# The seam between two transformer blocks, worked in two halves of the tokens

## The chip, the cores and the metric

The kernel runs on one core of a Trainium2 chip. The metric is the device time of one execution in microseconds (us), as the median of several runs. Five engines work side by side, each through its own instructions in a fixed order, and they wait for each other by semaphores: TensorE (PE: matmuls, and its weight loads, PEld), VectorE (DVE), ScalarE (ACT), GpSimd (POOL) and SyncE (SP, which here only starts transfers).

## The reference

Two blocks stand one behind the other, on 512 tokens of width 1024. Cut to what surrounds the seam:

```python
# end of the first block
x = x + 0.5 * swiglu(rmsnorm(x, ffn2_norm), ffn2_w_gate, ffn2_w_up, ffn2_w_down)
x = rmsnorm(x, final_norm)
# start of the second block
h = rms_norm(x, mix_pre_g) * (1.0 + sc_m) + sh_m
p = h @ w_in                     # 1024 -> 2848 columns
p_conv, p_rw = p[..., :2 * CONV_WIDTH], p[..., 2 * CONV_WIDTH:]
# ... shift by one token, and the low-rank products of tanh(wd), ad, sigmoid(gd)
```

`swiglu` ends in the "second down projection", 2816 -> 1024. `sc_m` and `sh_m` come from a modulation that is computed earlier.

## The kernel before

**Layout.** Activations lie transposed: features on the 128 partitions, the 512 tokens along the free axis, so `xT` is eight tiles of 128x512 (`KD = 8` row blocks). All products are made in three passes of split numbers (`passes`, lines 606 to 608: weight high by activation high, weight high by activation low, weight low by activation high), so each 128-deep step k of a row block costs three matmuls, each with a weight load of 128x128.

**Weights.** They come as slabs of 128x1024 through a ring of four (`RING`). SyncE starts the transfer of slab n when `slab_done` says that slab n-4 is used up. GpSimd splits each slab into `w_hi` (line 540) and `w_lo` (line 542) and signals `w_split`. A row block of the down projection takes three slabs (steps 0-7, 8-15, 16-21), a row block of the next projection ("in2", 23 row blocks) takes one.

**The seam.** `down("down2", ...)` (line 759) makes eight row blocks into banks 0 to 3 of PSUM in turn. VectorE adds each to `xT` (line 1829, `x_new`), ScalarE squares it (line 1329, and once more scaled by the final gain, line 1333), VectorE sums the squares (lines 1709 and 1714). The sums over features are taken by TensorE (`stat`, line 685). The two norms are folded: three sums per token give the factor of both norms together (`both_rs`) and that of the first alone (`n_rs`). Behind the last row block the chain is:

- TensorE `last_sums` with the squares of the last block; ScalarE two roots (lines 1373, 1374); VectorE two reciprocals (1720, 1722); TensorE `spread` (line 696), four transposes that lay `both_rs` over all partitions in bank 6;
- for each j of 8: VectorE scales `xT` (line 1754), ScalarE adds the shift and rounds to `h_hi` (line 1392), VectorE makes `h_lo` (line 1744), in a ping-pong over two tiles;
- TensorE `first(2, ...)` (lines 636, 637, 642) takes each j as it comes, for the first two slabs of in2, interleaved by k. Then it spreads `n_rs` into bank 5, and goes on with `project(2)`, `project(3)`, ...

```python
            first(2, at, "mixpre", lambda n: pe.wait_ge(S("x_new"), 21 + n))
            for m in range(2, 23):
                project(m)
                if 3 <= m <= 8:
                    lora_products(2 * (m - 3), 2 * (m - 3) + 2)
```

**Behind the seam.** The spread of `n_rs` lets VectorE finish the first norm in place (`final_norm`, line 2221, eight operations, `x_final`). Only then VectorE's fixed order comes to four memsets (2227) and the token shift of the first three row blocks (`shifted`, line 2014); ScalarE then applies tanh and two sigmoids (1627 to 1629, `lora_act`). The first low-rank product (line 1052), which stands in TensorE's order right behind `project(3)`, waits for both:

```python
                    if n == 0:
                        pe.wait_ge(S("lora_in"), 48)
                        pe.wait_ge(S("lora_act"), 3)
                        pe.wait_ge(S("masks_made"), 12)
                    ...
                    if n == 0:
                        pe.wait_ge(S("x_final"), 8)
```

The order of the work is written out by hand on every engine; nothing is planned at build time.

## Time and profile before

| | us |
|---|---|
| median of 3 runs (1737.14 to 1739.49) | 1737.27 |
| the profiled execution's own time | 1742.76 |
| its span | 1740.7 |
| PE busy | 1684.3 (97%) |
| POOL busy | 1017.7 (58%) |
| DVE busy | 976.7 (56%) |
| ACT busy | 428.6 (25%) |

The page's busy shares are means over a program of many stages. Of the slices (section 2 of the page), TensorE's granted clock stands at nine tenths or more nearly throughout, with three slices at eight tenths, none of them here. For this change one stretch of some 50 us matters, from the last row block of the down projection (its first matmul starts at 980.20) to the first low-rank product (1027.98). Times of the trace are counted from the start of the span.

### The profile page before, as it was taken

The numbers are of one execution on the slowest core, as the hardware profiler recorded it, in microseconds if no ns is written. First come the engines' busy times: TensorE is split into PE (matmuls) and PEld (weight loads), VectorE is DVE, ScalarE is ACT, GpSimd is POOL, SyncE is SP. The second block draws the span as 40 slices with busy tenths as digits, with TensorE's granted clock in tenths as the row PEclk, the third lists the DMA queues.
The fourth block names the chain that finished last, engine by engine and source line by source line (L and its number), as shares of the span: only waits on it lengthen the run. The fifth ranks groups of instructions, "written<-read, shape, count | busy, mean of one in ns | idle before, by whom it ended". The sixth has DMA issues, their size and how long they took to land.

```text
span 1740.7 us, 26685 instructions
## 1 busy us (share of the span) xinstructions
PE 1684.3 (97%) x10126; PEld 1363.6 (78%) x10126; DVE 976.7 (56%) x1413; ACT 428.6 (25%) x708; POOL 1017.7 (58%) x607
## 2 busy tenths in 40 slices
PE   8999999999989999999999999989999899999998
PEld 6888888887755678888888777878878788888886
DVE  6666661237566346566662269987746676556102
ACT  4000000017845321111100131323433333333001
POOL 3666667766576567666677644630005476666775
PEclk9999999999999999999999999999989899999998
DMA  6444443332220134444443322210002133323333
GB/s 214 156 145 144 145 145 109 99 125 91 79 68 2 37 104 145 145 145 145 145 157 99 107 84 73 94 40 3 3 2 85 61 97 96 96 96 96 105 101 109
DMA packets 49518, 173.76 MB, mean 100 GB/s; under 512 B 5632, under 2 KB 6016, under 8 KB 49312
## 3 DMA queue, kind: packets, MB, share of 16 engines
q1 hardware_dynamic: 40464, 143.00, 25.1%
q10 hardware_dynamic: 8976, 29.63, 5.3%
q8 instruction: 60, 0.98, 0.2%
q14 instruction: 18, 0.15, 0.0%
HBM read 170.51 MB, written 2.10 MB: 99 GB/s over the span
## 4 chain that ended last, share of the span: by engine, by line
PE 88%; DVE 5%; ACT 2%; POOL 2%; issue 1%; DMA 1%; SPq 0%; ACTq 0%; DVEq 0%; POOLq 0%
PE banks L606 24%; PE banks L608 24%; PE banks L607 24%; PE banks L1017 4%; PE banks L685 1%; POOL prob L549 1%; PE banks L917 1%; PE banks L636 1%; PE banks L903 1%; PE banks L642 1%; PE banks L637 1%; DMA w_raw<-in_slabs 1%; PE banks L992 1%; DVE tmp_r L1893 1%; PE banks L677 0%
## 5 line engine op out<-in xcount | busy, mean ns | idle before, releaser
L540 POOL TENSOR_SCALAR w_hi<-w_raw 128x1024 fp32r<-128x1024 f32 x260 | 294.2, 1131 | 645.6 <-DMA w_raw<-in_slabs 644.6
L542 POOL TENSOR_TENSOR w_lo<-w_raw,w_hi 128x1024 fp32r<-128x1024 f32 x260 | 643.0, 2473 | 21.7
L606 PE MATMUL banks<-h_hi,w_hi 128*128 128x512 f32 x1376 | 540.1, 392 | 2.3 <-POOL w_lo L542 2.3
L608 PE MATMUL banks<-h_hi,w_lo 128*128 128x512 f32 x1376 | 535.5, 389 | 0.0
L607 PE MATMUL banks<-h_lo,w_hi 128*128 128x512 f32 x1376 | 535.4, 389 | 0.0
L606 PEld LDWEIGHTS banks<-h_hi,w_hi 128*128 128x128 f32 x1376 | 258.3, 188 | 61.8 <-issue 5.8
L607 PEld LDWEIGHTS banks<-h_lo,w_hi 128*128 128x128 f32 x1376 | 258.3, 188 | 54.3 <-issue 1.7
L608 PEld LDWEIGHTS banks<-h_hi,w_lo 128*128 128x128 f32 x1376 | 258.3, 188 | 54.4
L606 PE MATMUL banks<-act_hi,w_hi 128*128 128x512 f32 x528 | 205.6, 389 | 0.0
L608 PE MATMUL banks<-act_hi,w_lo 128*128 128x512 f32 x528 | 205.4, 389 | 0.0
L607 PE MATMUL banks<-act_lo,w_hi 128*128 128x512 f32 x528 | 205.4, 389 | 0.0
L1781 DVE TENSOR_TENSOR act_lo<-tmp,act_hi 128x512 f32 x66 | 111.3, 1687 | 8.1
L608 PEld LDWEIGHTS banks<-act_hi,w_lo 128*128 128x128 f32 x528 | 99.1, 188 | 20.7
L607 PEld LDWEIGHTS banks<-act_lo,w_hi 128*128 128x128 f32 x528 | 99.1, 188 | 20.7
L606 PEld LDWEIGHTS banks<-act_hi,w_hi 128*128 128x128 f32 x528 | 99.1, 188 | 20.2
L1789 DVE TENSOR_TENSOR tmp<-banks,tmp 128x512 f32<-128x512 f32 x44 | 30.4, 692 | 149.5 <-PE banks L608 145.7
L1398 ACT ACTIVATE tmp<-tmp 128x512 f32<-128x512 f32 x44 | 27.9, 634 | 331.8 <-DVE tmp L1789 331.7
L1829 DVE SCALAR_TENSOR_TENSOR xT<-banks,xT 128x512 f32<-128x512 f32 x24 | 16.5, 690 | 164.2 <-PE banks L608 164.2
L549 POOL TENSOR_SCALAR prob<-prob,small 128x128 f32<-128x128 f32 (+3 forms) x64 | 69.4, 1100 | 27.0 <-DVE small L1967 26.8
L1803 DVE CUSTOM_DVE_ANT_0 adaw<-adaw,silc 128x1024 f32<-128x1024 f32 x48 | 78.2, 1629 | 5.6 <-DMA adaw<-in_ada 5.3
L2338 DVE SCALAR_TENSOR_TENSOR tmp<-banks,vec,tmp 128x511 f32<-128x511 f32 x44 | 32.8, 746 | 64.1 <-ACT tmp L1681 63.8
L1794 DVE TENSOR_TENSOR tmp<-tmp 128x512 f32<-128x512 f32 x44 | 62.1, 1410 | 8.5 <-ACT tmp L1398 8.5
(363 smaller groups left out, 1914.2 us busy)
## 6 DMA issues: line engine op xcount, KB each, us to landing
w_raw<-in_slabs SPq DMA_DIRECT2D x262, 512.0 KB, 3.5
adaw<-in_ada ACTq DMA_DIRECT2D x48, 512.0 KB, 3.7
relb<-in_relb ACTq DMA_DIRECT2D x8, 256.0 KB, 2.9
out_y<-xT SPq DMA_DIRECT2D x8, 256.0 KB, 2.1
w_raw<-in_slabs SPq DMA_DIRECT2D x4, 256.0 KB, 5.0
xT<-in_x SPq DMA_DIRECT2D x1, 1024.0 KB, 8.2
block<-in_block ACTq DMA_DIRECT2D x1, 704.0 KB, 6.2
xT<-in_x SPq DMA_DIRECT2D x2, 256.0 KB, 3.7
```

The lines of the kernel that those rows point to most:

```text
L540: nc.gpsimd.tensor_scalar(w_hi[:, r, :], w_raw[:, r, :], 1.0, 1.0, ALU.mult, ALU.mult).then_inc(S("w_hi"), 1)
L542: nc.gpsimd.tensor_tensor(w_lo[:, r, :], w_raw[:, r, :], w_hi[:, r, :], ALU.subtract).then_inc(S("w_split"), 1)
L549: nc.gpsimd.tensor_scalar(p, p, of_step(row_sum, t)[:, e:e + 1], None, ALU.mult).then_inc(S("probs_normed"), 1)
L606: mm(out, hi, rhs_hi, start=start, stop=False, skip_group_check=True)
L607: mm(out, hi, rhs_lo, start=False, stop=False, skip_group_check=True)
L608: return mm(out, lo, rhs_hi, start=False, stop=stop, skip_group_check=True)
L1017: last = mm(out, block_of(lhs, operands, e, g, c), r, start=opens and i == 0, stop=i == len(pairs) - 1, skip_group_check=True)
L1781: v.tensor_tensor(actl_t[:, bass.ds(at * T, T)], t, hi, ALU.subtract).then_inc(S("act_lo"), 1)
L1789: v.tensor_tensor(tmp[:, 2 + u, :], bank[2 * u], tmp[:, 0, :], ALU.mult).then_inc(S("gate_scaled"), 1)
L1794: v.tensor_tensor(tmp[:, 4 + u, :], tmp[:, 2 + u, :], tmp[:, 4 + u, :], ALU.mult)\
L1803: v.tensor_tensor_reduce(out=adaw[:, u, :], in0=adaw[:, u, :], in1=silc, scale=1.0, scalar=0.0, op0=ALU.mult, op1=ALU.add, accum_out=mod_s ...
L2338: v.scalar_tensor_tensor(out=tmp[:, n, 1:T], in0=bank[n][:, 0:T - 1], scalar=w[1], in1=tmp[:, n, 1:T], op0=ALU.mult, op1=ALU.add).then_inc ...
```

## The change

The last row block of the down projection, the norm chain and the first three slabs of in2 are worked for tokens 0-255 first and for tokens 256-511 after them.

- TensorE: `last_row_of_down2` makes the row block as two halves (bank 3 and bank 2), each with all 22 steps, with the statistics and the spread of half 0 put between the steps of half 1. `first_of_in2` makes slabs 0, 1, 2 for half 0, slab behind slab, with the statistics and the spread of half 1 in slab 0, and then slabs 0, 1, 2 for half 1. The ring's `slab_done` comes only in the second half of each. The spread of `n_rs` stands behind all six. `project` begins with m = 3.
- VectorE: `pre_halves` runs scale and `h_lo` by halves (16 pairs for 8), with the sum (`pre_sum`) and the root (`pre_root`) of half 1 between those of half 0.
- ScalarE: squares, roots and `h_hi` by halves; the start of two small transfers stands between `h_hi` of half 0 and of half 1.
- Semaphore counts behind it are shifted by one (`root_of`, `squares_before`, ...); no other work moves.

The core of the diff:

```diff
@@ TensorE @@
+            def last_tile_sums(half):
+
+                pe.wait_ge(S("norm_square"), squares_before("mixpre") + 8 + half)
+                for t in (2 * half, 2 * half + 1):
+                    last = mm(bank[7][:, 3 * t:3 * t + 3], tmp[:, 1, P * t:P * t + P], of_last, start=False, stop=True,
+                              skip_group_check=True)
+                last.then_inc(S("norm_stat"), 1)
+
+            def both_spread(half):
+
+                pe.wait_ge(S("both_rs"), half + 1)
+                for t in (2 * half, 2 * half + 1):
+                    last = nc.tensor.transpose(bank[6][:, P * t:P * t + P], both_rs[:, t:t + 1].to_broadcast([P, P]), ident)
+                last.then_inc(S("second_mm"), 1)
+
+            def last_row_of_down2():
+
+                def part(half, s, k0, k1):
+                    n = SLAB_AT["down2"] + 3 * (KD - 1) + s
+                    return product(bank[3 - half][:, tokens_of(half)], n, n % RING, act_hi, act_lo, ks=range(k0, k1), start=k0 == 0,
+                                   stop=k1 == KF, at_slab=k0 - DOWN_CUT[s][0], tokens=tokens_of(half))
+
+                pe.wait_ge(S("x_new"), 16 + KD - 4)
+                part(0, 0, 0, 8)
+                part(0, 1, 8, 16)
+                part(0, 2, 16, KF - 1)
+                sums_of_most("mixpre")
+                part(0, 2, KF - 1, KF).then_inc(S("half_mm"), 1)
+                pe.wait_ge(S("x_new"), 16 + KD - 1)
+                part(1, 0, 0, 4)
+                last_tile_sums(0)
+                part(1, 0, 4, 6)
+                both_spread(0)
+                part(1, 0, 6, 8).then_inc(S("slab_done"), 1)
+                part(1, 1, 8, 16).then_inc(S("slab_done"), 1)
+                part(1, 2, 16, KF).then_inc(S("slab_done"), 1)
+
+            def first_of_in2(at):
+
+                def part(half, n, k0, k1):
+                    for k in range(k0, k1):
+                        if k == 0:
+                            if half == 0:
+                                pe.wait_ge(S("x_new"), 25 if n == 2 else 21 + n)
+                            pe.wait_ge(S("w_split"), at + n + 1)
+                        done = 8 * (HI_AT["mixpre"] + half) + k + 1
+                        w, r, out = slice(P * k, P * k + P), (at + n) % RING, bank[n][:, tokens_of(half)]
+                        pe.wait_ge(S("norm_hi"), done)
+                        mm(out, w_hi[:, r, w], h_hi[:, k, tokens_of(half)], start=k == 0, stop=False, skip_group_check=True)
+                        mm(out, w_lo[:, r, w], h_hi[:, k, tokens_of(half)], start=False, stop=False, skip_group_check=True)
+                        pe.wait_ge(S("norm_lo"), done)
+                        last = mm(out, w_hi[:, r, w], h_lo[:, k, tokens_of(half)], start=False, stop=k == KD - 1, skip_group_check=True)
+                    return last
+
+                part(0, 0, 0, 3)
+                last_tile_sums(1)
+                part(0, 0, 3, 6)
+                both_spread(1)
+                part(0, 0, 6, 8)
+                part(0, 1, 0, 8)
+                part(0, 2, 0, 8)
+                for n in range(3):
+                    part(1, n, 0, 8).then_inc(S("slab_done"), 1)
+                pe.wait_ge(S("norm_rs"), root_of("mixpre") + 1)
+                spread(bank[5], n_rs, 1).then_inc(S("norm_spread"), 1)
...
-            first(2, at, "mixpre", lambda n: pe.wait_ge(S("x_new"), 21 + n))
-            for m in range(2, 23):
+            first_of_in2(at)
+            for m in range(3, 23):
                 project(m)
@@ ScalarE @@
+            pre_square(0)
+            pre_std(0)
+            pre_hi(0, range(6))
+            pre_square(1)
+            pre_hi(0, (6,))
+            pre_std(1)
+            pre_hi(0, (7,))
             for i in range(2):
                 act.dma_start(lora[:, i, :], lora_in[:, i, :]).then_inc(S("lora_in"), 16)
-            norm_hi("mixpre")
+            pre_hi(1, range(KD))
@@ VectorE @@
+            def pre_halves():
+
+                sum_squares("mixpre", 6)
+                pre_sum(0)
+                pre_root(0)
+                for half in range(2):
+                    pre_scaled(half, 0)
+                    pre_scaled(half, 1)
+                    for j in range(KD):
+                        pre_lo(half, j)
+                        if j + 2 < KD:
+                            pre_scaled(half, j + 2)
+                        if half == 0 and j == 3:
+                            pre_sum(1)
+                        if half == 0 and j == 5:
+                            pre_root(1)
+                dve.wait_ge(S("norm_std"), root_of("mixpre") + 1)
+                v.reciprocal(n_rs, n_std).then_inc(S("norm_rs"), 2)
...
-            norm_split("mixpre", gs["mixpre"])
+            pre_halves()
```

How the instructions move. First place, TensorE, the start of in2. The names are PSUM banks, the split activations (`h_hi`, `h_lo`) and the split slab (`w_hi`, `w_lo`). Before:

```order
L696 MATMUL banks<-both,small 128x128 [waits both_rs]
L696 MATMUL banks<-both,small 128x128 x3
L636 MATMUL banks<-h_hi,w_hi 128x512 [waits norm_hi,w_split,x_new]
L637 MATMUL banks<-h_hi,w_lo 128x512
L636 MATMUL banks<-h_hi,w_hi 128x512 [waits w_split,x_new]
L637 MATMUL banks<-h_hi,w_lo 128x512
L642 MATMUL banks<-h_lo,w_hi 128x512 [waits norm_lo]
L642 MATMUL banks<-h_lo,w_hi 128x512
```

Now, from step k = 2 of slab 0, half 0:

```order
L786 MATMUL banks<-h_hi,w_hi 128x256 [waits norm_hi]
L787 MATMUL banks<-h_hi,w_lo 128x256
L789 MATMUL banks<-h_lo,w_hi 128x256 [waits norm_lo]
L742 MATMUL banks<-small,tmp 128x3 [waits norm_square]
L742 MATMUL banks<-small,tmp 128x3
L786 MATMUL banks<-h_hi,w_hi 128x256 [waits norm_hi]
L787 MATMUL banks<-h_hi,w_lo 128x256
L789 MATMUL banks<-h_lo,w_hi 128x256 [waits norm_lo]
```

Before, each step served two slabs with six matmuls of 512 columns behind one pair of waits; now a step serves one slab with three matmuls of 256 columns, and the statistics of half 1 stand among them.

Second place, TensorE, around the spread of `n_rs` (line 696 before, 706 now). Before:

```order
L642 MATMUL banks<-h_lo,w_hi 128x512
L696 MATMUL banks<-both,small 128x128 [waits norm_rs]
L696 MATMUL banks<-both,small 128x128 x3
L606 MATMUL banks<-h_hi,w_hi 128x512 [waits w_split]
L607 MATMUL banks<-h_lo,w_hi 128x512
L608 MATMUL banks<-h_hi,w_lo 128x512
```

Now:

```order
L789 MATMUL banks<-h_lo,w_hi 128x256 [waits norm_lo]
L706 MATMUL banks<-both,small 128x128 [waits norm_rs]
L706 MATMUL banks<-both,small 128x128 x3
L618 MATMUL banks<-h_hi,w_hi 128x512 [waits w_split]
L619 MATMUL banks<-h_lo,w_hi 128x512
L620 MATMUL banks<-h_hi,w_lo 128x512
```

Before, 48 matmuls (slabs 2 and 3) stood between the spread and the first low-rank product; now 24 do (slab 3), since slab 2 stands ahead of the spread.

Third place, VectorE, the middle of half 0 (scale at line 1867, `h_lo` at 1874, the sum of half 1 at 1850). Now:

```order
L1874 SCALAR_TENSOR_TENSOR h_lo<-tmp,mod,h_hi 128x256 [waits norm_hi]
L1867 SCALAR_TENSOR_TENSOR tmp<-xT,mod,banks 128x256 [waits norm_lo]
L1850 SCALAR_TENSOR_TENSOR xT<-banks,xT 128x256 [waits slab_done]
L1874 SCALAR_TENSOR_TENSOR h_lo<-tmp,mod,h_hi 128x256 [waits norm_hi]
L1867 SCALAR_TENSOR_TENSOR tmp<-xT,mod,banks 128x256 [waits norm_lo]
```

The sum of half 1 waits for the end of the down projection, and four `h_lo` of half 0 (with two scalings between them) are still behind it in VectorE's order, the first of them j = 4. Before, no such wait stood inside the sequence.

## Rows read from the trace of the kernel before

**Rows 1.** the page: busy time by engine, and the chain that ended last.
```profile
PE 1684.3 (97%) x10126; PEld 1363.6 (78%) x10126; DVE 976.7 (56%) x1413; ACT 428.6 (25%) x708; POOL 1017.7 (58%) x607
...
PE 88%; DVE 5%; ACT 2%; POOL 2%; issue 1%; DMA 1%; SPq 0%; ACTq 0%; DVEq 0%; POOLq 0%
```

**Rows 2.** stretches: us, busy of PE, PEld, DVE, ACT, POOL, then PEclk, DMA.
```profile
980.20:1016.07 35.87, 32.19 (x143) 25.80 (x142) 17.36 (x26) 7.93 (x14) 17.09 (x10) 0.90 0.24 74
1000.40:1007.20 6.80, 5.11 (x14) 3.35 (x13) 5.82 (x7) 2.22 (x4) 3.42 (x2) 0.50 0.23 77
1050.90:1100.00 49.10, 49.10 (x203) 37.97 (x203) 47.99 (x74) 5.66 (x9) 25.93 (x16) 1.00 0.23 76
```

**Rows 3.** TensorE in time: start us, us, engine, line, tiles, shape, count [idle].
```profile
994.02 0.39 PE L607 MATMUL banks<-act_lo,w_hi 128*128 128x512 f32 x1
994.25 0.39 PE L608 MATMUL banks<-act_hi,w_lo 128*128 128x512 f32 x1
994.48 1.84 PE L685 MATMUL banks<-small,tmp 128*128 128x2 f32 x16
996.18 0.49 PE L606 MATMUL banks<-act_hi,w_hi 128*128 128x512 f32 x1
...
998.58 1.05 PE L685 MATMUL banks<-small,tmp 128*128 128x3 f32 x8 [1.44 <-ACT tmp L1329]
...
1002.83 0.77 PE L636 MATMUL banks<-h_hi,w_hi 128*128 128x512 f32 x1 [1.69 <-ACT h_hi L1392]
...
1016.07 0.60 PE L696 MATMUL banks<-both,small 128*128 128x128 f32 x4
...
1021.98 0.39 PE L606 MATMUL banks<-h_hi,w_hi 128*128 128x512 f32 x1
...
1027.98 0.70 PE L1052 MATMUL banks<-in_arena 64*128 64x512 f32 x2 [0.40 <-issue]
```

**Rows 4.** TensorE in time, attention stage: two and three transposes.
```profile
505.02 0.44 PE L903 MATMUL banks<-both,prob 128*128 128x128 f32 x2
...
559.75 0.55 PE L903 MATMUL banks<-both,prob 128*128 128x128 f32 x3
```

**Rows 5.** VectorE in time order, around the seam.
```profile
1002.72 2.10 DVE L1744 SCALAR_TENSOR_TENSOR h_lo<-tmp,mod,h_hi 128x512 fp32r<-128x512 f32 x1
...
1005.52 0.75 DVE L1744 SCALAR_TENSOR_TENSOR h_lo<-tmp,mod,h_hi 128x512 fp32r<-128x512 f32 x1
...
1006.97 0.75 DVE L1744 SCALAR_TENSOR_TENSOR h_lo<-tmp,mod,h_hi 128x512 fp32r<-128x512 f32 x1
...
1016.77 5.36 DVE L2221 SCALAR_TENSOR_TENSOR xT<-xT,vec,banks 128x512 f32<-128x512 f32 x8 [1.97 <-PE banks L696]
1022.09 0.56 DVE L2227 MEMSET in_arena<- 128x32 f32 x4
1022.68 1.41 DVE L2014 SCALAR_TENSOR_TENSOR in_arena<-banks,vec,in_arena 128x511 f32<-128x511 f32 x2
1024.01 0.74 DVE L2014 SCALAR_TENSOR_TENSOR tmp<-banks,vec,tmp 128x511 f32<-128x511 f32 x1
```

**Rows 6.** GpSimd in time order: the two halves of one slab split.
```profile
1000.77 1.04 POOL L540 TENSOR_SCALAR w_hi<-w_raw 128x1024 fp32r<-128x1024 f32 x1 [2.28 <-DMA w_raw<-in_slabs]
1001.90 2.37 POOL L542 TENSOR_TENSOR w_lo<-w_raw,w_hi 128x1024 fp32r<-128x1024 f32 x1
```

**Rows 7.** groups by shape: busy us, mean ns, idle; one operation, two widths.
```profile
L1958 DVE CUSTOM_DVE_ANT_0 prob<-banks,relb 128x512 f32<-128x512 f32 x8 | 5.2, 688 | 2.6 <-PE banks L883 2.6
...
L1958 DVE CUSTOM_DVE_ANT_0 prob<-banks,relb 128x256 f32<-128x256 f32 x8 | 3.1, 422 | 0.1
```

**Rows 8.** ScalarE in time order, before the first low-rank product.
```profile
1024.78 0.64 ACT L1627 ACTIVATE in_arena<-in_arena 64x512 f32<-64x512 f32 x1 [0.61 <-DVE tmp L2014]
...
1027.27 0.61 ACT L1629 ACTIVATE tmp<-tmp 128x512 f32<-128x512 f32 x1
```

**Rows 9.** the page: slab transfers, count, size, median us to landing.
```profile
w_raw<-in_slabs SPq DMA_DIRECT2D x262, 512.0 KB, 3.5
```

More of the change, by code:

```diff
@@ L344, in build @@
         mod_sum = small_t[:, 236:237]
-        pre_ms, pre_std, pre_rs = (small_t[:, 24 + 4 * i:28 + 4 * i] for i in range(3))
+        pre_ms, pre_std_at, pre_rs = (small_t[:, 24 + 4 * i:28 + 4 * i] for i in range(3))
         gain_q = small_t[:, 200:203]
@@ L608, in passes, with product @@
                 return mm(out, lo, rhs_hi, start=False, stop=stop, skip_group_check=True)
-            def product(out, n, r, act_h, act_l, ks=range(KD), first=0, start=True, stop=True, wait_k=None, at_slab=0):
+            def product(out, n, r, act_h, act_l, ks=range(KD), first=0, start=True, stop=True, wait_k=None, at_slab=0,
+                        tokens=slice(None)):
                 pe.wait_ge(S("w_split"), n + 1)
@@ L619, in product @@
                     a, b = start and i == 0, stop and i == len(ks) - 1
-                    last = passes(out, hi, lo, act_h[:, first + k, :], act_l[:, first + k, :], a, b)
+                    last = passes(out, hi, lo, act_h[:, first + k, tokens], act_l[:, first + k, tokens], a, b)
                 return last
@@ L648, in first @@
                     norm_stats(late)
-                elif norm == "mixpre":
-                    pe.wait_ge(S("norm_rs"), NORMS.index(norm) + 1)
-                    spread(bank[5], n_rs, 1).then_inc(S("norm_spread"), 1)
             def first_loaded(wait_bank):
@@ L727, in norm_spread @@
             def norm_spread(name):
-                q = NORMS.index(name)
+                q = root_of(name) - 1
                 pe.wait_ge(S("norm_rs"), q + 1)
@@ L761, in down @@
                 at = SLAB_AT[name]
-                for m in range(KD):
+                for m in range(KD - 1 if norm == "mixpre" else KD):
                     if m >= 4:
@@ L772, in down @@
                         wait_k = (lambda k: pe.wait_ge(S("act_lo"), o + 3 + k)) if m == 0 else None
-                        early = norm in ("mixpre", "ffnpost") and m == KD - 1 and s == 2
+                        early = norm == "ffnpost" and m == KD - 1 and s == 2
                         if early:
@@ L782, in down @@
                     return
+                if norm == "mixpre":
+                    last_row_of_down2()
+                    return
                 last_sums(norm)
-                if norm == "mixpre":
-                    pe.wait_ge(S("both_rs"), 1)
-                    spread(bank[6], both_rs, 1).then_inc(S("second_mm"), 1)
-                else:
-                    norm_spread(norm)
+                norm_spread(norm)
             gate_up("gu1", 0, "ffn1")
@@ L1329, in square @@
                     f(tmp[:, j % 2 if j else 4, :], at, ACT.Square).then_inc(S("norm_square"), 1)
-                    if name == "mixpre" and j < KD - 1:
+                    if name == "mixpre":
                         if j >= 3:
@@ L1357, in norm_squares @@
                 else:
-                    for j in range(KD):
+                    for j in range(KD - 1 if name == "mixpre" else KD):
                         if name == "ffn2" and j == KD - 1:
@@ new lines, in pre_root, with pre_scaled @@
+            def pre_root(half):
+                cols = slice(2 * half, 2 * half + 2)
+                dve.wait_ge(S("second_std"), half + 1)
+                v.reciprocal(both_rs[:, cols], both_std[:, cols]).then_inc(S("both_rs"), 1)
+            def pre_scaled(half, j):
+                h, n = slice(HALF * half, HALF * half + HALF), 8 * (HI_AT["mixpre"] + half)
+                if j == 0:
+                    dve.wait_ge(S("second_mm"), half + 1)
+                    dve.wait_ge(S("x_new"), 16 + KD + half)
+                if j >= 2:
+                    dve.wait_ge(S("norm_lo"), n + j - 1)
+                v.scalar_tensor_tensor(out=tmp[:, 4 + j % 2, h], in0=xT[:, j, h], scalar=gs["mixpre"][:, j:j + 1], in1=bank[6][:, h],
+                                       op0=ALU.mult, op1=ALU.mult).then_inc(S("norm_t"), 1)
@@ new lines, in pre_lo @@
+            def pre_lo(half, j):
+                h = slice(HALF * half, HALF * half + HALF)
+                dve.wait_ge(S("norm_hi"), 8 * (HI_AT["mixpre"] + half) + j + 1)
+                v.scalar_tensor_tensor(out=h_lo[:, j, h], in0=tmp[:, 4 + j % 2, h], scalar=shf["mixpre"][:, j:j + 1],
+                                       in1=h_hi[:, j, h], op0=ALU.add, op1=ALU.subtract).then_inc(S("norm_lo"), 1)
+            def pre_halves():
[15 more added lines that the diff above has]
+                v.reciprocal(n_rs, n_std).then_inc(S("norm_rs"), 2)
+                dve.wait_ge(S("norm_rs"), root_of("mixpre") + 1)
@@ L1824, in add_half @@
             def add_half(o, at, n_slabs, scale, norm):
-                for m in range(KD):
+                for m in range(KD - 1 if norm == "mixpre" else KD):
                     sum_squares(norm, m - 1)
@@ L2315, in _ @@
             post_scaled(0)
-            dve.wait_ge(S("norm_std"), NORMS.index("ffnpre") + 1)
-            v.reciprocal(pre_rs, pre_std).then_inc(S("norm_rs"), 1)
+            dve.wait_ge(S("norm_std"), root_of("ffnpre"))
+            v.reciprocal(pre_rs, pre_std_at).then_inc(S("norm_rs"), 1)
             post_added(0)
```

90 lines of the change are left out of this document (49 added, 41 removed).

## The prediction

> **What bounds the kernel now.** The page first: TensorE is busy for 97% of the span and carries 88% of the chain that ended last [rows 1]. So a change pays only where TensorE waits, runs at the lower clock, or does less; it does not do less here. The views of stretches and of time around the seam show what there is to win. From 980.20 (last row block of the down projection) to the spread at 1016.07 TensorE is busy 32.2 of 35.9 us, and from 1000.40 to 1007.20 its granted clock is 0.50, that is 1.2 instead of 2.4 GHz, behind a gap in which it had only the short statistics and four transposes to do [rows 2, 3]. Between the row block's end (three matmuls from 996.18) and the first matmul of in2 (1002.83) lie about 5.9 us; the matmuls from 1002.83 to 1007.20 ran at the lower clock, which cost half of 4.4, so 2.2. About 7 us is the most that halves can win.
>
> Next the reader is to look behind the seam. The first low-rank product starts at 1027.98 with 0.40 idle ahead of it [rows 3]. It waits for VectorE: spread at 1016.07, final norm 1016.77 to 1022.09, four memsets, three shifts to 1024.75 [rows 5], then tanh from 1024.78 and two sigmoids, of which the last ends at 1027.88 [rows 8]. That chain is 11.91 us long from the spread on, and TensorE has just enough to do meanwhile: four transposes and two slabs. It has no slack.
>
> **The change, part by part.**
>
> *Matmul count and pitch.* 66 (22 steps) and 72 (three slabs of 8) matmuls of 512 columns become 276 of 256 columns, with as many weight loads. At 512 columns one starts every 0.227: two starts are 0.23 apart, and 24 x 0.227 + 4 x 0.11 = 5.89 of the 5.91 us between 1016.07 and 1021.98 [rows 3]. No row has 256 columns with a full weight load. From below: half of it is 0.113, and a weight load with next to nothing behind it already takes 0.106 (16 in 996.18 - 994.48 = 1.70) [rows 3], with a transpose 0.11 (0.55 for three less 0.44 for two) [rows 4]. From above: 512 columns at 2.4 GHz are 0.213; if the surplus of 0.013 comes with each matmul, 256 columns take 0.107 + 0.013 = 0.120. I take the middle, 0.117: 276 x 0.117 = 32.3 for 138 x 0.227 = 31.3, so +1.0 (0 to +1.8).
>
> A rule speaks against that. The rows show a weight load hidden under the matmul before it: load alone 0.106, matmul alone 0.213, together 0.227 [rows 3]. The Trainium skill, "TensorE: Matmul & The Clock Gate", section "What overlaps and what doesn't", says that a weight load overlaps matmuls in flight only where the row groups differ; here they are the same, so the trace disagrees at 512 columns, and what is left of it is the rival below. The same page's section "Back-to-back issue gap" gives N/2.4 + 2.5 ns: by it 256 columns take an estimated 0.109, and the sum would be 276 x 0.109 = 30.1, 2.2 less than mine; at 512 columns it gives 0.216, and the rows have 0.227.
>
> *Statistics and spreads.* 16 + 4 + 4 weight-load pairs x 0.111 = 2.7 and 4 transposes x 0.11 = 0.4: the same number as before, at other places.
>
> *The spread of n_rs with no wait at all.* 980.20 + 32.3 + 2.7 + 0.4 = 1015.6. It must stand behind all three slabs now; before, it stood behind two, at 1016.07. So even a perfect overlap moves it by only -0.5 (-1.5 to +0.3 with the pitch).
>
> *Waits in slab 0.* Half 0 of the row block ends at 980.2 + 7.7 + 1.8 + 0.3 = 989.9 or so; sum, square, statistics, root and spread at half width put the first h_lo at about 994. Before, one h_lo followed another by 1.45 (1005.52 to 1006.97) [rows 5]. Half width saves 0.27 on each of the two operations (688 to 422 ns) [rows 7], so 0.92; h_lo 0 to 3 are there by 997, while TensorE ends half 1 at 998.3. Up to here the plan works.
>
> Then GpSimd comes in. Before, it stood still from 1004.3 on, since slabs were released late. Now the three slabs of the row block are released in half 1: the first at 993.4, and 3.5 (transfer [rows 9]) + 0.2 later, at 997.1, GpSimd begins slab 1 of in2. A split takes 1.04 + 2.37 + gaps = 3.5 [rows 6]: slab 1 to 1000.6, slab 2 to 1004.4, slab 3 to 1008.2, without a pause. What that does to VectorE is in one pair of rows: the h_lo of 1002.72 took 2.10 instead of 0.75 [rows 5]; GpSimd's operation ran from 1001.90 to 1004.27 [rows 6], and h_lo ended 0.55 after it. An operation of VectorE that reads two tiles in SBUF waits until GpSimd's current one has ended (the scalings, which read PSUM too, do not). So from 998 on one h_lo passes for each operation of GpSimd. h_lo 4, which also stands behind the sum of half 1 (998.8), ends at 1000.9; h_lo 5 behind the first part of slab 2's split, 1002.1; h_lo 6 behind its second part, 1004.7; h_lo 7, 1005.9. TensorE, in strict order k by k, waits 0.65, 0.8, 0.45 (for the spread of half 1, whose reciprocal stands behind scaling 7), 1.45 and 0.8, and 0.2 later, with some 0.5 for starting again: 4.9. Bounds: 0, if VectorE is never held up; 5.4 with transfers 0.2 later. Slabs 1 and 2 of half 0 and all of half 1 then run through: VectorE ends half 1 at 1014.6, and TensorE comes to it at 1012.
>
> Sum: 1015.6 + 4.9 = 1020.5 for the spread, +4.4.
>
> *Behind the spread.* The chain of 11.91 is untouched and now starts at 1020.5: first low-rank product at 1032.4, for 1027.98. TensorE has only slab 3 to do meanwhile (0.44 + 5.44 = 5.9) and stands idle for 6.0. That third slab ahead of the spread is the step which decides: what it brought forward on TensorE is given back in full.
>
> *Clock.* A gap of 5.9 with a little work in it was followed by the lower clock [rows 2]; one of 6.0 with none will be too. The fall lasted 6.8; if half of that lies under matmuls, it costs 1.7 (0 to 3.4). A fall in slab 0, where TensorE is busy for about a third of 5 us, would cost some 1.7; I put one in four on it, 0.4.
>
> *Costs nothing.* The transfers of the low-rank weights start 3.6 later on ScalarE's queue and are wanted at 1032; their 0.8 on that queue lies between h_hi 7 of half 0 and the first of half 1, which waits for VectorE anyway. Slab 4's transfer starts at 1015, wanted at 1032. SyncE's queue holds only slabs, in the old order.
>
> *Does it reach the end?* From 1050.90 to 1100.00 TensorE is busy 49.10 of 49.10 and VectorE 47.99 [rows 2]. VectorE's long convolution work begins with a gate that comes from slabs 3 and 4, so it is late by the same amount. Nothing absorbs it.
>
> Total: 4.4 + 1.7 + 0.4 = +6.5. The profiled execution took 1742.76 and would take 1749.3; the median of the runs is 5.5 lower: 1737.27 + 6.5 = 1743.8.
>
> **The rivals.**
>
> *VectorE is not held up (the other side: not slower).* If h_lo keeps its 0.92, h_lo 7 is there near 1001.5, slab 0 runs through, and the spread comes at 1014.6 to 1015.6. With the clock's 1.7 that is +0.2 to +1.2, about 1738. It decides from the point where GpSimd's split of slabs 1 and 2 lies clear of h_lo 4 to 7. For it: both engines' operations are short, and VectorE may catch the pauses of 0.1. Against it: the 2.10. Chance 0.13.
>
> *The low-rank product doesn't wait.* Then slab 3 sets the shift: 1020.5 + 0.44 - 1021.98 = -1.0, 1736.7. Against it: the 0.40 idle and the end of the last sigmoid 0.10 ahead of it. Chance 0.03.
>
> *The clock costs more.* The gap brings 6.8 us of lower clock all under matmuls, and one fall comes in slab 0: 4.4 + 3.4 + 1.7 = +9.5, 1746.8. Chance 0.14.
>
> *The weight load isn't hidden at 256 columns.* Pitch 0.106 + 0.113 = 0.22 instead of 0.117: 276 x 0.103 = 28.4 more, less the 4.9 of waits that it would hide: +30, 1767. Against it: transposes at 0.11 with a full load each [rows 4]. The Trainium skill's overlap rule, named above, would make it so. Chance 0.05.
>
> **How the numbers follow.** The likeliest (0.65) is 1743.8, alone 1741 to 1747. A difference under 0.2% (3.5 us) is about what a measurement can't tell from none. Slower: 0.61 + 0.14 + 0.05 = 0.80. Same: 0.11 of the first rival, 0.02 of the second, 0.04 of the likeliest's low end, 0.17. Faster: 0.03. The range is 1738.5 to 1748.0: below it a part of the first two rivals, above it the last and a part of the third.
>
> **What would show it.** Pitch: two starts of 256-column matmuls 0.113 to 0.120 apart. Lock: h_lo operations of over 1 us between 998 and 1009, ending 0.3 behind one of GpSimd's. Behind the spread: TensorE idle for about 6 us ahead of the low-rank product, 11.9 behind the spread, and a clock of 0.50 right after. It is wrong if that gap is under 3 us, if h_lo run at 0.5 throughout, or if the 256-column pitch is over 0.13.

## The result and the profile after

The changed kernel is slower. In the first measurement its median is 1746.24 us (1744.77 to 1747.25, 6 runs) against 1737.98 (1737.14 to 1739.49, 6 runs) of the kernel before: ratio 1.0042, 95% interval 1.0030 to 1.0054, or +7.3 us (5.2 to 9.4); the medians lie 8.3 apart. Measured again beside the experiments below: 1746.71 against 1739.11, ratio 1.0036 (1.0019 to 1.0053). Forecast were 1743.8 (1738.5 to 1748.0) and "slower" with 0.80. One run of experiment 1 below took 2411 us at a mean granted clock of 0.65 and is left out of its ratio.

The profiled execution took 1747.25 us (span 1745.3). First its busy times and chain of waits, as [rows 1]:

```profile
PE 1687.5 (97%) x10264; PEld 1372.0 (79%) x10264; DVE 973.5 (56%) x1431; ACT 431.1 (25%) x719; POOL 1019.2 (58%) x607
...
PE 90%; DVE 4%; ACT 2%; POOL 2%; issue 1%; DMA 1%; SPq 0%; ACTq 0%; DVEq 0%; POOLq 0%
```

138 matmuls more, TensorE 3.2 us more busy. Now TensorE in time order through the seam, as [rows 3] (L618 to L620 the row block, L742 statistics, L786 to L789 the halves of in2, L750 and L706 spreads, L1128 the low-rank products):

```profile
995.82 0.28 PE L618 MATMUL banks<-act_hi,w_hi 128*128 128x256 f32 x1
995.94 0.28 PE L619 MATMUL banks<-act_lo,w_hi 128*128 128x256 f32 x1
...
1002.20 0.38 PE L789 MATMUL banks<-h_lo,w_hi 128*128 128x256 f32 x1 [0.29 <-DVE h_lo L1874]
1002.79 0.43 PE L750 MATMUL banks<-both,small 128*128 128x128 f32 x2 [0.21 <-DVE small L1857]
...
1006.05 0.43 PE L789 MATMUL banks<-h_lo,w_hi 128*128 128x256 f32 x1 [1.86 <-DVE h_lo L1874]
1006.27 0.41 PE L786 MATMUL banks<-h_hi,w_hi 128*128 128x256 f32 x1
...
1022.14 0.60 PE L706 MATMUL banks<-both,small 128*128 128x128 f32 x4
...
1034.04 2.08 PE L1128 MATMUL banks<-in_arena 64*128 64x512 f32 x4 [5.81 <-ACT tmp L1732]
```

The reader is to see three things. Two starts of 256-column matmuls are 0.120 apart at 2.4 GHz (and 0.214 at 1.2 GHz: the fifteenth behind 1006.27 starts at 1009.48). The spread of n_rs stands at 1022.14 instead of 1016.07. And ahead of the first low-rank product TensorE is idle for 5.81, where it was 0.40. The stretches, as [rows 2]:

```profile
980.20:1022.14 41.94, 39.33 (x306) 38.16 (x305) 25.09 (x44) 11.83 (x27) 18.77 (x12) 0.96 0.28 88
1006.25:1009.67 3.42, 3.42 (x17) 3.42 (x17) 3.21 (x3) 0.91 (x2) 3.03 (x2) 0.50 0.00 0
1028.30:1034.04 5.74, 0.00 (x0) 0.03 (x1) 2.32 (x6) 3.06 (x4) 4.61 (x4) 0.96 0.30 93
1033.56:1040.39 6.83, 6.35 (x14) 4.00 (x15) 0.00 (x0) 1.65 (x3) 1.77 (x1) 0.50 0.00 0
1056.95:1106.05 49.10, 49.10 (x202) 37.21 (x201) 47.60 (x73) 7.52 (x12) 24.80 (x15) 1.00 0.26 84
```

TensorE stood idle for 2.6 of the 41.9 us up to the spread. The lower clock came twice, and the second time 6.35 of its 6.83 us lie under matmuls. Further on TensorE is busy throughout again, as before. Then VectorE, as [rows 5], and GpSimd, as [rows 6], both in time order:

```profile
996.04 0.48 DVE L1874 SCALAR_TENSOR_TENSOR h_lo<-tmp,mod,h_hi 128x256 fp32r<-128x256 f32 x1
...
999.24 1.99 DVE L1874 SCALAR_TENSOR_TENSOR h_lo<-tmp,mod,h_hi 128x256 fp32r<-128x256 f32 x1
...
1001.66 0.48 DVE L1874 SCALAR_TENSOR_TENSOR h_lo<-tmp,mod,h_hi 128x256 fp32r<-128x256 f32 x1
...
1002.65 3.34 DVE L1874 SCALAR_TENSOR_TENSOR h_lo<-tmp,mod,h_hi 128x256 fp32r<-128x256 f32 x2
...
1006.96 2.68 DVE L1874 SCALAR_TENSOR_TENSOR h_lo<-tmp,mod,h_hi 128x256 fp32r<-128x256 f32 x1 [0.18 <-ACT h_hi L1488]
```

```profile
998.56 2.39 POOL L554 TENSOR_TENSOR w_lo<-w_raw,w_hi 128x1024 fp32r<-128x1024 f32 x1
1002.18 1.04 POOL L552 TENSOR_SCALAR w_hi<-w_raw 128x1024 fp32r<-128x1024 f32 x1 [1.23 <-DMA w_raw<-in_slabs]
1003.31 2.40 POOL L554 TENSOR_TENSOR w_lo<-w_raw,w_hi 128x1024 fp32r<-128x1024 f32 x1
...
1006.98 2.38 POOL L554 TENSOR_TENSOR w_lo<-w_raw,w_hi 128x1024 fp32r<-128x1024 f32 x1
```

Each held-up h_lo ends 0.28 behind an operation of GpSimd: 999.24 + 1.99 = 1001.23 behind 1000.95, 1002.65 + 3.34 = 1005.99 behind 1005.71, 1006.96 + 2.68 = 1009.64 behind 1009.36. The one at 1001.66 ran free: GpSimd was waiting for a transfer from 1000.95 to 1002.18. The row of 3.34 holds two: TensorE took the first of them at 1003.55, behind the end of GpSimd's operation at 1003.22.

### The profile page after: what moved, and what is told of

Same layout as the page of the kernel before. It is cut to its first block, busy times and chain, and to the rows that moved or that the text cites. A ratio compares the mean times of both kernels' runs of the same rounds, so it can differ in the third digit from the quotient of the medians.

```text
span 1745.3 us, 26997 instructions
## 1 busy us (share of the span) xinstructions
PE 1687.5 (97%) x10264; PEld 1372.0 (79%) x10264; DVE 973.5 (56%) x1431; ACT 431.1 (25%) x719; POOL 1019.2 (58%) x607
## 4 chain that ended last, share of the span: by engine, by line
PE 90%; DVE 4%; ACT 2%; POOL 2%; issue 1%; DMA 1%; SPq 0%; ACTq 0%; DVEq 0%; POOLq 0%
PE banks L618 24%; PE banks L620 24%; PE banks L619 24%; PE banks L1093 4%; POOL prob L561 1%; PE banks L695 1%; PE banks L993 1%; PE banks L979 1%; PE banks L649 1%; PE banks L655 1%; PE banks L650 1%; DMA w_raw<-in_slabs 1%; PE banks L964 1%; PE banks L968 1%; PE banks L687 0%
## 5 line engine op out<-in xcount | busy, mean ns | idle before, releaser
L618 PE MATMUL banks<-h_hi,w_hi 128*128 128x512 f32 x1368 | 538.1, 393 | 2.7 <-POOL w_lo L554 2.6
L620 PE MATMUL banks<-h_hi,w_lo 128*128 128x512 f32 x1368 | 533.2, 390 | 0.0
L618 PEld LDWEIGHTS banks<-h_hi,w_hi 128*128 128x128 f32 x1368 | 257.3, 188 | 63.2 <-issue 7.3
L620 PEld LDWEIGHTS banks<-h_hi,w_lo 128*128 128x128 f32 x1368 | 257.2, 188 | 54.0
L618 PE MATMUL banks<-act_hi,w_hi 128*128 128x512 f32 (+1 forms) x550 | 209.6, 381 | 0.0
L620 PE MATMUL banks<-act_hi,w_lo 128*128 128x512 f32 (+1 forms) x550 | 209.3, 381 | 0.0
L619 PE MATMUL banks<-act_lo,w_hi 128*128 128x512 f32 (+1 forms) x550 | 209.3, 381 | 0.0
L618 PEld LDWEIGHTS banks<-act_hi,w_hi 128*128 128x128 f32 x550 | 103.4, 188 | 19.8
L619 PEld LDWEIGHTS banks<-act_lo,w_hi 128*128 128x128 f32 x550 | 103.4, 188 | 19.7
L620 PEld LDWEIGHTS banks<-act_hi,w_lo 128*128 128x128 f32 x550 | 103.4, 188 | 19.6
L1918 DVE TENSOR_TENSOR act_lo<-tmp,act_hi 128x512 f32 x66 | 107.2, 1625 | 8.1
```

The costliest lines, as they stand in the source:

```text
L618: mm(out, hi, rhs_hi, start=start, stop=False, skip_group_check=True)
L619: mm(out, hi, rhs_lo, start=False, stop=False, skip_group_check=True)
L620: return mm(out, lo, rhs_hi, start=False, stop=stop, skip_group_check=True)
L1918: v.tensor_tensor(actl_t[:, bass.ds(at * T, T)], t, hi, ALU.subtract).then_inc(S("act_lo"), 1)
```

## The experiments

Each was timed in five rounds of runs; runs of the kernel before stand beside each group, so that a ratio has an interval of some +-0.15% (2.6 us). The seam itself is read more sharply in a trace, from VectorE's sum of the seventh row block to the first key norm's product, 19 slabs later (three of the last row block and 16 of in2). Before and after (the other kernels are read in the same way):

```profile
980.39 0.69 DVE L1829 SCALAR_TENSOR_TENSOR xT<-banks,xT 128x512 f32<-128x512 f32 x1 [9.65 <-PE banks L608]
```
```profile
1105.25 1.02 PE L1064 MATMUL banks<-tmp,block 128*128 128x512 f32 x2
```
```profile
980.63 0.69 DVE L1966 SCALAR_TENSOR_TENSOR xT<-banks,xT 128x512 f32<-128x512 f32 x1 [9.81 <-PE banks L620]
```
```profile
1114.27 1.02 PE L1140 MATMUL banks<-tmp,block 128*128 128x512 f32 x2
```

124.9 before, 133.6 after: the seam is 8.8 us longer. How far two single traces can be apart by chance is seen in kernel 5: there nothing of this stretch is edited, and it takes 0.8 more than before, with a clock of 0.50 from 1004.4 to 1014.4 instead of for 6.8 us. Differences of under 1 us in the last column are therefore not read.

| kernel | median us | ratio to before (95%) | as us | seam against before, trace |
|---|---|---|---|---|
| after, again | 1746.71 | 1.0036 (1.0019 to 1.0053) | +6.3 | +8.7 |
| 1 early spread | 1739.48 | 1.0001 (0.9988 to 1.0014) | +0.2 | +1.8 |
| 2 two slabs | 1741.53 | 1.0017 (0.9999 to 1.0035) | +3.0 | +1.8 |
| 3 PSUM tiles | 1741.08 | 1.0017 (1.0004 to 1.0031) | +3.0 | +3.1 |
| 4 busy gap | 1744.57 | 1.0025 (1.0013 to 1.0037) | +4.3 | +6.1 |
| 5 pitch (before, seven row blocks in halves) | 1745.8 | 1.0036 (1.0021 to 1.0051) | +6.3 | +0.8 (its edit lies ahead of the stretch) |
| 6 low-rank products later | 1739.94 | 1.0003 (0.9989 to 1.0016) | +0.5 | +1.4 |
| 7 early spread and PSUM tiles | 1733.27 | 0.9966 (0.9952 to 0.9979) | -5.9 | -5.2 |
| 8 before with PSUM tiles | 1737.8 | 1.0001 (0.9989 to 1.0014) | +0.2 | -0.3 |
| 9 before with PSUM tiles, early spread | 1737.63 | 1.0000 (0.9989 to 1.0010) | 0.0 | +0.2 |

**The changed kernel again.**

> The changed kernel once more, beside the others. Theory A (the time is made at the seam: waits for VectorE in slab 0, the spread of n_rs behind three slabs, an idle TensorE of 5.8 us ahead of the first low-rank product and the lower clock behind it): slower than before by 7 to 9 us, first low-rank product at 1034 in the trace (before 1028), and the shift at 1040 near +9. Theory B (half of it is given back behind 1150, as the two traces read): slower by 4 to 5 us.

The median is +7.6 and the ratio +6.3 (3.3 to 9.2), so theory A is within the interval and B not excluded by it. The trace decides: in this second one the shift against before's trace is +8.7 at 1043 (low-rank products) and +9.0 at the end of the span (1749.7 to 1740.7). What the first pair seemed to give back behind 1150 isn't given back here. The reason is told further down.

**1. The spread of n_rs early** (line 1894 moves into the loop, TensorE's spread behind slab 0 of half 1):

```
-                for n in range(3):
-                    part(1, n, 0, 8).then_inc(S("slab_done"), 1)
-                pe.wait_ge(S("norm_rs"), root_of("mixpre") + 1)
-                spread(bank[5], n_rs, 1).then_inc(S("norm_spread"), 1)
+                for n in range(3):
+                    part(1, n, 0, 8).then_inc(S("slab_done"), 1)
+                    if n == 0:
+                        pe.wait_ge(S("norm_rs"), root_of("mixpre") + 1)
+                        spread(bank[5], n_rs, 1).then_inc(S("norm_spread"), 1)
...
+                        if half == 0 and j == 7:
+                            dve.wait_ge(S("norm_std"), root_of("mixpre") + 1)
+                            v.reciprocal(n_rs, n_std).then_inc(S("norm_rs"), 2)
```

> The changed kernel with the reciprocal of n_rs taken behind the last h_lo of half 0 and its spread put between slab 0 and slab 1 of half 1, instead of behind slab 2. Theory A (what decides is that the spread stands behind the third slab): spread at about 1016.4, first low-rank product at 1028.3 instead of 1034.0, idle ahead of it under 0.5 instead of 5.8, no lower clock at 1033 to 1040; about 8 us faster than the changed kernel, within 0 to +1.5 us of the kernel before. Rival (the chain behind the spread is bound by something else, such as the shifts, which need slab 2): low-rank product at 1031 or later and 4 us or less gained.

TensorE in time order, and a stretch:

```profile
1017.32 0.60 PE L706 MATMUL banks<-both,small 128*128 128x128 f32 x4
...
1029.23 1.13 PE L1129 MATMUL banks<-in_arena 64*128 64x512 f32 x4
```
```profile
1005.08:1011.91 6.83, 6.32 (x30) 6.10 (x29) 6.50 (x13) 2.78 (x6) 2.84 (x2) 0.50 0.04 16
```

No idle ahead of the low-rank product, and 11.91 from spread to product as ever. It is 7 us faster than the changed kernel, where theory A said about 8. Both marks are 0.9 later than expected, although this trace's seam begins 0.8 earlier, so 1.7 us are to be explained: the lower clock in slab 0 lasted 6.8 instead of 3.4, and 30 instead of 16 matmuls lay under it, which is 1.3 of them. The place of the spread is the step that decides. The edit doesn't touch the waits in slab 0, and they are still there.

**2. Two slabs in halves**, the third in full width behind the spread:

```
-                part(0, 2, 0, 8)
-                for n in range(3):
+                for n in range(2):
...
-            for m in range(3, 23):
+            for m in range(2, 23):
```

> The changed kernel with two slabs of in2 in halves; the third is done in full width behind the spread, as in the kernel before. Theory A: half 1 comes earlier to TensorE (about 1010.6), which then waits for VectorE's h_lo at 0.92 apiece; spread at about 1018.9, low-rank product at 1030.8, idle ahead of it about 0.6, no lower clock behind it; +2.8 us against the kernel before, 5 to 6 faster than the changed kernel. Rival (the cost lies in the halves and not in the third slab): +7 to +9 against before, as the changed kernel.

```profile
1018.35 0.60 PE L706 MATMUL banks<-both,small 128*128 128x128 f32 x4
...
1030.26 1.13 PE L1127 MATMUL banks<-in_arena 64*128 64x512 f32 x4 [0.38 <-issue]
```

Spread and product are near the marks, and no lower clock follows (1.00 from 1030.26 to 1045). The seam is +1.8 by the trace, the time +3.0 (-0.2 to 6.1). Theory A; the rival (+7 to +9) lies outside the interval.

**3. The scaled half tiles in PSUM**, so that h_lo (and h_hi) read a bank:

```
-                v.scalar_tensor_tensor(out=tmp[:, 4 + j % 2, h], in0=xT[:, j, h], ...
+                v.scalar_tensor_tensor(out=bank[(4, 3)[j % 2]][:, h], in0=xT[:, j, h], ...
...
-                v.scalar_tensor_tensor(out=h_lo[:, j, h], in0=tmp[:, 4 + j % 2, h], ...
+                v.scalar_tensor_tensor(out=h_lo[:, j, h], in0=bank[(4, 3)[j % 2]][:, h], ...
```

> The changed kernel with the scaled half tiles in two free PSUM banks instead of SBUF, so that h_lo reads one tile in SBUF and one in PSUM. Theory A (an operation of VectorE that reads two tiles in SBUF waits for the end of GpSimd's current one): no h_lo over 0.6 us, slab 0 of half 0 without the waits of about 3 us, no lower clock at 1006 to 1009.7, spread at about 1017.5 instead of 1022.1, low-rank product at 1029.4; idle ahead of it still near 6 and the lower clock behind it still there; 3 to 5 us faster than the changed kernel. Rival (VectorE is held up whatever it reads, or the long h_lo are waits for ScalarE): as the changed kernel, within 1 us.

GpSimd and VectorE over the same time:

```profile
999.91 2.39 POOL L554 TENSOR_TENSOR w_lo<-w_raw,w_hi 128x1024 fp32r<-128x1024 f32 x1
...
1003.59 2.41 POOL L554 TENSOR_TENSOR w_lo<-w_raw,w_hi 128x1024 fp32r<-128x1024 f32 x1
```
```profile
1000.54 0.47 DVE L1874 SCALAR_TENSOR_TENSOR h_lo<-banks,mod,h_hi 128x256 fp32r<-128x256 f32 x1
...
1004.41 0.48 DVE L1874 SCALAR_TENSOR_TENSOR h_lo<-banks,mod,h_hi 128x256 fp32r<-128x256 f32 x1 [0.15 <-ACT h_hi L1488]
```
```profile
981.93 0.69 DVE L1966 SCALAR_TENSOR_TENSOR xT<-banks,xT 128x512 f32<-128x512 f32 x1 [9.71 <-PE banks L620]
```
```profile
1018.15 0.60 PE L706 MATMUL banks<-both,small 128*128 128x128 f32 x4
...
1030.05 2.08 PE L1128 MATMUL banks<-in_arena 64*128 64x512 f32 x4 [5.81 <-ACT tmp L1732]
```

With one input in PSUM every h_lo takes 0.47 to 0.48 in the middle of GpSimd's 2.4 us operations, while GpSimd splits the same slabs. From the seventh sum to the spread it is 1018.15 - 981.93 = 36.2 us, against 1022.14 - 980.63 = 41.5 in the changed kernel: 5.3 less. The idle of 5.81 and the lower clock behind it are untouched, as expected. So it is shown that VectorE is held up, and by which operands.

**4. The gap filled** with 22 matmuls of 512 columns, whose result the first low-rank product overwrites:

```
+                if m == 3:
+                    pe.wait_ge(S("x_final"), 1)
+                    for _ in range(22):
+                        mm(bank[4], h_hi[:, 1, 0:P], h_hi[:, 0, :], start=True, stop=True, skip_group_check=True)
```

> The changed kernel with 22 matmuls of 512 columns, whose result is overwritten unread, put behind the fourth slab of in2, into the 5.8 us in which TensorE waits for the low-rank product (22 x 0.227 = 5.0). Theory A (of the shift of 9 us, 6 are the wait and 3 the lower clock behind it): low-rank product unchanged at 1034.0, granted clock 1.00 from 1034 to 1041, shift at 1040 +6 instead of +9; 3 us faster than the changed kernel. Rival (the clock falls all the same or its cost is hidden by VectorE further on): within 1 us of the changed kernel.

```profile
1028.41 5.15 PE L1336 MATMUL banks<-h_hi 128*128 128x512 f32 x22
1034.38 1.13 PE L1128 MATMUL banks<-in_arena 64*128 64x512 f32 x4 [0.82 <-issue]
```
```profile
1034.38:1041.15 6.77, 6.76 (x28) 4.73 (x29) 0.00 (x0) 1.27 (x2) 1.26 (x1) 1.00 0.00 0
```

The product is within 0.4 of where it was, the clock stays at 1.00, and the seam is 2.7 shorter (+6.1 for +8.8). So the lower clock behind the gap costs 2.7 by the trace; the timed difference of 2 us (4.3 for 6.3) agrees, within wide intervals.

**5. The pitch alone**: the kernel before with rows 0 to 6 of the second down projection in halves. Both halves of a row block are summed in one bank, in turn slab by slab, and this kernel doesn't give the reference's results; which step of it spoils the sums wasn't looked into. It serves for the time alone: the number and the size of its instructions are those of correct halves.

```
+                        if norm == "mixpre" and m < KD - 1:
+                            for h in (slice(0, T // 2), slice(T // 2, T)):
+                                last = product(bank[m % 4][:, h], n, n % RING, act_hi, act_lo, ks=range(k0, k1),
+                                               start=s == 0, stop=s == 2, wait_k=wait_k, tokens=h)
```

> The kernel BEFORE with the first seven row blocks of the second down projection in halves of the tokens: 462 matmuls of 512 columns become 924 of 256. Theory A (a fixed surplus of 0.013 with every matmul: 0.120 at 256 columns, 0.227 at 512): 462 x 0.013 = +6.0 us against the kernel before. Rival 1 (0.117, as predicted): +3.2. Rival 2 (half of the width is half of the time): 0. Rival 3 (the weight load shows): +48.

VectorE's sums behind two row blocks, here and in the kernel before:

```profile
970.85 0.69 DVE L1836 SCALAR_TENSOR_TENSOR xT<-banks,xT 128x512 f32<-128x512 f32 x1 [12.00 <-PE banks L608]
986.69 0.69 DVE L1836 SCALAR_TENSOR_TENSOR xT<-banks,xT 128x512 f32<-128x512 f32 x1 [11.89 <-PE banks L608]
```
```profile
965.43 0.69 DVE L1829 SCALAR_TENSOR_TENSOR xT<-banks,xT 128x512 f32<-128x512 f32 x1 [10.72 <-PE banks L608]
```

A row block takes 15.84 instead of 14.96 (980.39 - 965.43), that is 132 x 0.120 for 66 x 0.227; seven of them 6.2. The seventh sum comes 6.3 later than before (986.69 for 980.39), and the timed runs give +6.3 (3.7 to 8.9). Theory A; 0.117 would have made it 3.2. The rows carry this reading more than the runs do: six of the twelve runs took 1741.2 to 1743.7 us and six 1747.9 to 1751.5, for a reason told further down.

**6. Low-rank products one slab later**:

```
-                if 3 <= m <= 8:
-                    lora_products(2 * (m - 3), 2 * (m - 3) + 2)
+                if 4 <= m <= 9:
+                    lora_products(2 * (m - 4), 2 * (m - 4) + 2)
```

> The changed kernel with every pair of low-rank products one slab later (behind slab 4 instead of slab 3, and so on). Theory A (what costs is that TensorE has nothing to do for 5.8 us): TensorE waits 1.3 for the shift that frees bank 0, then does slab 4 and finds the low-rank product's inputs ready; no lower clock; shift at 1042 +2 to +3, 5 to 8 us faster than the changed kernel. Rival (VectorE, late by 6 us, bounds what follows): 0 to 3 us faster, with waits of TensorE for VectorE in 1040 to 1150 instead.

```profile
1023.16 0.60 PE L706 MATMUL banks<-both,small 128*128 128x128 f32 x4
...
1030.58 0.50 PE L618 MATMUL banks<-h_hi,w_hi 128*128 128x512 f32 x1 [1.33 <-DVE in_arena L2151]
...
1036.24 1.13 PE L1128 MATMUL banks<-in_arena 64*128 64x512 f32 x4
```

The wait of 1.33 is as worked out, no lower clock follows, and 6 to 7 us come back although VectorE's chain is as late as in the changed kernel (spread at 1023.16). So behind the seam it is TensorE's lost time that counts, not VectorE's lateness; the rival (0 to 3 us faster) falls.

**7. Both edits of 1 and 3.**

> The changed kernel with both edits: the spread of n_rs between slab 0 and slab 1 of half 1, and the scaled half tiles in PSUM. Theory A: no waits in slab 0 (spread at 1012 or so), low-rank product at about 1024, idle ahead of it under 1, no lower clock between 1003 and 1050: 4 us faster than the kernel before, 12 faster than the changed kernel. Rival (behind the seam VectorE bounds the convolution stage, so that TensorE's gain doesn't reach the end): 0 to 2 us faster than the kernel before.

```profile
1009.72 0.60 PE L706 MATMUL banks<-both,small 128*128 128x128 f32 x4
...
1021.64 1.13 PE L1129 MATMUL banks<-in_arena 64*128 64x512 f32 x4
```
```profile
980.00:1050.00 70.00, 69.90 (x442) 60.01 (x441) 44.79 (x85) 22.68 (x43) 40.13 (x23) 1.00 0.29 92
```

It beats both kernels: 0.9966 (0.9952 to 0.9979) of the kernel before, 5.9 us (3.7 to 8.3), where 4 were expected; the spread, expected at 1012 or so, came at 1009.72, and this trace's seam begins 1.1 earlier than before's. TensorE is busy for 69.90 of 70.00 us at full clock.

**8 and 9. The kernel before with the same edits, without halves**: the scaled tiles in banks 4 and 3 (8), and besides the spread of n_rs right behind the first norm's (9):

```
-                    v.scalar_tensor_tensor(out=tmp[:, 4 + j % 2, :], in0=xT[:, j, :], ...
+                    v.scalar_tensor_tensor(out=bank[(4, 3)[j % 2]], in0=xT[:, j, :], ...
...
                     spread(bank[6], both_rs, 1).then_inc(S("second_mm"), 1)
+                    pe.wait_ge(S("norm_rs"), NORMS.index(norm) + 1)
+                    spread(bank[5], n_rs, 1).then_inc(S("norm_spread"), 1)
```

> The kernel BEFORE (no halves) with the scaled tiles of this norm in two free PSUM banks instead of SBUF, so that h_lo reads one tile in SBUF. Theory A (the lock costs the kernel before only one held-up h_lo, 2.10 instead of 0.75 at 1002.72, and the gap and the lower clock behind it stay): no h_lo over 0.8 us, spread at 1014.7 to 1016, -1 us against before (0 to -1.4). Rival (the gain of the kernel with both edits, -5.4 us against before, comes from the PSUM tiles and not from the halves): -4 to -6.

> The kernel BEFORE with the same PSUM tiles, and besides with the spread of n_rs put right behind the spread of the first norm's root, into the time in which TensorE waits for h_hi. Theory A: four transposes (0.44) leave the path and the final norm starts when VectorE is free, at 1013 instead of 1016.8; the 0.40 ahead of the low-rank product goes; TensorE has nothing more to gain, so -2 us against before (-1 to -2.5), and -5 needs the halves. Rival (an early spread is worth by itself what it brought the changed kernel, 7 us): -6 or more.

Neither changes the time: 1.0001 (0.9989 to 1.0014) and 1.0000 (0.9989 to 1.0010). In 8 no h_lo takes over 0.75, as expected. The expected -1 lies within the interval of 8 (seam -0.3), the -2 at the edge of that of 9 (seam +0.2), so for 9 I probably overrated the edit; in its trace the lower clock lasted 10.2 us (998.5 to 1008.7) instead of 6.8. Whether the eight transposes that now stand in the gap made it longer isn't shown: in kernel 5, which has four there as before, it lasted 10 us as well. Both rivals (-4 or more) are excluded. The two edits are worth nothing measurable to full-width tiles and some 12 us to half-width ones (1.0036 to 0.9966): the gain of kernel 7 needs the halves.

## Why the prediction was right, point by point

**Direction and mechanism.** Right: slower, by the third slab ahead of the spread (by the medians experiments 1, 2 and 6 take back 7.2, 5.2 and 6.8 us of it) and by GpSimd's hold on VectorE (3). The step that failed in size is the clock.

**Pitch.** 0.120, the upper bound, where I took 0.117: at 2.4 GHz the surplus of 0.013 comes with each matmul, at 256 columns as at 512; at 1.2 GHz none is seen (0.214 apart, for 0.213 of columns). +1.8 instead of +1.0 (5). The Trainium skill's "Back-to-back issue gap" ("TensorE: Matmul & The Clock Gate") gives N/2.4 + 2.5 ns, an estimated 0.109 here; the rows have 0.120, so its surplus is a fifth of the measured one, at both widths. But the section gives that formula for a matmul by itself; for a stream of load and matmul pairs, which this is, it has 131 ns at 512 columns, and the rows have 227. The rule on overlap that the prediction took from the same page, which made the rival with the load not hidden (0.22 apart), is refuted at 256 columns too.

**Waits in slab 0.** Without any wait the spread would have come at 980.43 + 276 x 0.120 + 2.66 + 0.44 = 1016.65 (the row block began 0.2 later here); it came 5.5 later. Of these, 2.6 are idle (1.86 of it ahead of 1006.05), 1.5 the lower clock (16 matmuls at 0.214 instead of 0.120), which I had put at one in four and 0.4, and 1.4 are left: restarts behind each wait, and waits that the profile doesn't list as idle, since the matmul before them is still counted as busy (1001.29 stands 0.43 behind its forerunner at 1000.86). So waits with restarts took 4.0 where 4.9 stood. The mechanism was right, the phases were not: slab 2 of in2 landed later, GpSimd paused from 1000.95 to 1002.18, and h_lo 5 slipped through free. h_lo 6 came at about 1003.5 for 1004.7; that h_lo 7 ended at 1005.99, for 1005.9 forecast, by other phases than those worked out, owes something to luck. Experiment 3 takes back 5.3 of the 5.5 with the lock.

That VectorE waits for the whole of GpSimd's operation is in the rows above, and experiment 3 shows on which operands it depends. The Trainium skill, "SBUF — State Buffer", section "Who interferes with whom", states it as a rule: the two engines share a pair of ports, and an operation of VectorE with two inputs in SBUF contends with one of GpSimd that reads SBUF, and one with at most one such input doesn't, outside special modes. The traces agree: up to 2.68 with two, 0.48 with one.

So the rival in which VectorE isn't held up falls; its spread at 1014.6 to 1015.6 wasn't reached even with the hold-up gone (3: 36.2 behind the seventh sum, which is 1016.85 in the changed kernel's time), since the pitch and the late start alone give 1016.65.

**Behind the spread.** 11.90 from spread to product (forecast 11.91), idle 5.81 (6.0): right.

**Clock behind the gap.** Forecast 1.7, with 3.4 as the bound; 6.35 us of it lay under matmuls, which cost 2.7 by experiment 4. This term was mis-sized: half of a stretch was put under matmuls, but the fall began 0.5 ahead of the first matmul behind the gap. So both conditions of the rival "the clock costs more" came true, a fall in slab 0 and one behind the gap nearly all under matmuls. What happened at the seam (+8.8) is that rival (+9.5), to which I had given 0.14, and not the likeliest course (0.65).

**A slip.** The rival in which the low-rank product doesn't wait has -1.0 and 1736.7; its own sum gives 1737.27 - 1.0 = 1736.3, and 1736.7 only with the clock's 0.4 added, which it doesn't say. Nothing else hangs on it.

**"Nothing absorbs it."** The first pair of traces spoke against it: at the end of the span the shift was only 4.6 (1745.3 to 1740.7). It was a chance of the two executions, at one place. Between 1140 and 1160 VectorE makes factors for the recurrence with operations on two SBUF tiles, in the time of GpSimd's last splits. TensorE's wait for it and the clock behind it, in before, after, and after again:

```profile
1150.72 1.11 PE L992 MATMUL banks<-both,in_arena 128*128 128x128 f32 x4 [3.19 <-DVE in_arena L2014]
```
```profile
1157.77 2.81 PE L1068 MATMUL banks<-both,in_arena 128*128 128x128 f32 x24 [0.78 <-DVE in_arena L2151]
```
```profile
1159.38 1.11 PE L1068 MATMUL banks<-both,in_arena 128*128 128x128 f32 x4 [3.13 <-DVE in_arena L2151]
```
```profile
1159.36:1162.78 3.42, 3.11 (x14) 2.74 (x15) 2.64 (x5) 0.60 (x1) 3.02 (x2) 0.50 0.00 0
```

Before's VectorE and GpSimd just ahead of it:

```profile
1145.04 1.53 DVE L2097 TENSOR_TENSOR in_arena<-in_arena 128x512 f32<-128x512 f32 x1
1146.49 2.84 DVE L2098 TENSOR_TENSOR in_arena<-in_arena 128x512 f32<-128x512 f32 x1
```
```profile
1144.63 1.40 POOL L540 TENSOR_SCALAR w_hi<-w_raw 128x1024 fp32r<-128x1024 f32 x1 [2.78 <-DMA w_raw<-in_slabs]
1146.11 2.67 POOL L542 TENSOR_TENSOR w_lo<-w_raw,w_hi 128x1024 fp32r<-128x1024 f32 x1
```

The longest wait there is either 0.8 or 3.0 to 3.3. In the traces it goes with which of VectorE's operations meet GpSimd's (here two that take 0.69 when free); no edit tested that. Where the wait is the long one the lower clock follows. Of the twelve traces five have it (before, after again, 4, 5, 9), and from the key norm to the end of the span they take 634.6 to 636.9 us, the seven others 629.8 to 632.2. That no edit decides it is seen in the two traces of the changed kernel, one on either side. It fits the 5.5 us by which the profiled execution of before lay over its median. How often each kernel draws it in timed runs, which have no trace, stays open. Of the 90 runs of before beside the experiments 18 took over 1742.4 us, of kernel 5 six of twelve over 1747.9; if these are the long wait, a median of twelve runs can be off by a us or more by the draw alone, and the column of traces is the surer one. So the step holds for the seam's 8.8 us: where both traces have the long wait, all of it is there at the end.

**Size.** +6.5 forecast, +8.8 at the seam, +7.3 (5.2 to 9.4) in the runs. Against the terms: clock 1.5 + 2.7 for 2.1, pitch +0.8, waits -0.9; that is +2.0, and 0.3 stay unexplained, less than two traces differ by chance. At the seam the forecast was 2.3 too small, most of it the clock; that the timed +7.3 lies nearer to it is within its interval of 4 us.
